# The opening of a diffusion mixer layer on one core: order of the first loads, and of TensorE's first steps

## The reference, cut to what matters

```
mod = silu(c) @ w_ada + b_ada                 # w_ada is (1024, 3072); one row for latent, one for context
shift, scale, gate = split(mod, 3)
h = rmsnorm(x, rms_g) * (1 + scale) + shift   # x is (tokens, 1024)
q, k, v, z_a, glu, z_b, gates = split(h @ w_in + b_in)
```

## Time and profile before

| | |
|---|---|
| median of 3 runs | 1721.22 us (1721.03 to 1722.77) |
| the profiled execution | 1720.91 us, of which its span is 1719.3 us |
| PE busy in the span | 1700.5 us (99%) |
| DVE, ACT, POOL busy | 1244.4, 866.7 and 653.4 us |
| granted clock of PE, mean | 0.999 |
| start of the first main product (line 1845) | 85.04 us |

### The profile page before, as it was taken

One profiled execution on the slowest core, in us unless ns is written; L12 is line 12 of the kernel. 1 busy time (PEld: TensorE's weight loads), 2 busy tenths in 40 slices (PEclk: granted clock), 3 DMA queues, 4 the chain that ended last, 5 costly groups with the idle time before them and its releaser, 6 DMA issues.

```text
span 1719.3 us, 27684 instructions
## 1 busy us (share of the span) xinstructions
PE 1700.5 (99%) x9909; PEld 1444.6 (84%) x9909; DVE 1244.4 (72%) x1791; ACT 866.7 (50%) x1508; POOL 653.4 (38%) x509
## 2 busy tenths in 40 slices
PE   8999999999999999999999999999999999999998
PEld 5787888888899988888888888888988888888886
DVE  3785888788757758887677856777777655678776
ACT  3553434454576644444554436777779222433443
POOL 0044676565200027865555653224223100015443
PEclk9999999999999999999999999999999999999999
DMA  9453534333598735444333369997666777673452
GB/s 325 127 158 118 140 122 145 92 89 111 182 325 247 212 92 141 156 120 111 99 129 99 110 169 220 245 209 192 167 143 173 247 239 227 195 258 133 150 159 86
DMA packets 271644, 286.31 MB, mean 167 GB/s; under 512 B 49960, under 2 KB 217748, under 8 KB 268309
## 3 DMA queue, kind: packets, MB, share of 16 engines
q1 hardware_dynamic: 271106, 284.18, 55.9%
q10 hardware_dynamic: 403, 0.37, 0.1%
HBM read 203.18 MB, written 81.30 MB: 165 GB/s over the span
## 4 chain that ended last, share of the span: by engine, by line
PE 94%; DMA 2%; DVE 1%; SPq 1%; issue 1%; POOL 1%; ACT 0%; POOLq 0%; DVEq 0%; ACTq 0%
PE banks L1845 45%; PE banks L2399 6%; PE banks L2974 4%; PE banks L2976 4%; PE banks L2975 4%; PE banks L3034 3%; PE banks L3036 3%; PE banks L3035 3%; PE banks L2363 3%; PE banks L1973 2%; PE banks L1975 2%; PE banks L1974 2%; PE banks L2369 2%; DMA w_ada<-in_w_ada 1%; PE banks L2339 1%; PE banks L2340 1%
## 5 line engine op out<-in xcount | busy, mean ns | idle before, releaser
L1845 PE MATMUL banks<-a_hi,w_hi 128*128 128x512 f32 x1176 | 460.7, 392 | 0.7 <-ACT out_stage L1122 0.4
L1845 PE MATMUL banks<-a_hi,w_lo 128*128 128x512 f32 x1176 | 458.3, 390 | 0.0
L1845 PE MATMUL banks<-a_lo,w_hi 128*128 128x512 f32 x1176 | 458.1, 390 | 0.0
L1514 DVE SCALAR_TENSOR_TENSOR banks<-glu_out,taps,banks 128x1009 f32<-128x1009 f32 (+1 forms) x240 | 342.2, 1426 | 5.2
L1845 PEld LDWEIGHTS banks<-a_hi,w_hi 128*128 128x128 f32 x1176 | 220.9, 188 | 50.0 <-issue 3.6
L1845 PEld LDWEIGHTS banks<-a_hi,w_lo 128*128 128x128 f32 x1176 | 220.9, 188 | 46.0
L1845 PEld LDWEIGHTS banks<-a_lo,w_hi 128*128 128x128 f32 x1176 | 221.0, 188 | 45.0
L1005 POOL TENSOR_TENSOR t_raw<-w_raw 128x512 f32<-128x512 f32 x39 | 53.8, 1380 | 397.7 <-DMA w_raw<-in_w_in 391.5
L1433 DVE SCALAR_TENSOR_TENSOR w_lo<-w_raw,w_hi 128x1024 fp32r<-128x1024 f32 x84 | 108.9, 1296 | 103.9 <-ACT w_hi L1096 102.6
L959 POOL TENSOR_TENSOR w_lo<-t_raw,w_hi 128x1024 fp32r<-128x1024 f32 x70 | 171.6, 2461 | 25.7 <-ACT w_hi L1096 23.3
L2511 ACT ACTIVATE probs<-scores,stat 128x640 f32<-128x640 f32 (+2 forms) x128 | 106.7, 833 | 52.3 <-DVE stat L2433 50.9
(11 more groups left out here) (286 smaller groups left out, 3687.5 us busy)
## 6 DMA issues: line engine op xcount, KB each, us to landing
w_raw<-in_w_in SPq DMA_DIRECT2D x34, 1024.0 KB, 5.6
cw_raw<-in_w_in SPq DMA_DIRECT2D x44, 512.0 KB, 5.0
proj<-out_stage SPq DMA_DIRECT2D x80, 256.0 KB, 2.3
gates_in<-proj SPq DMA_DIRECT2D x64, 256.0 KB, 3.0
k_hi<-k_hi_rows SPq DMA_DIRECT2D x16, 640.0 KB, 10.8
k_lo<-k_lo_rows SPq DMA_DIRECT2D x16, 640.0 KB, 13.3
q_split<-q_rows SPq DMA_DIRECT2D x8, 1152.0 KB, 6.2
w_ada<-in_w_ada SPq DMA_DIRECT2D x8, 1024.0 KB, 11.2
```

The costliest lines, as they stand in the source:

```text
L1514: op = dve.scalar_tensor_tensor(dst, src, by, dst, ALU.mult, ALU.add)
L1845: op = pe.matmul(out, x[w][:, b, k], y, start=(start and k == j == 0), stop=(k == H - 1 and j == 2), skip_group_check=not start)
```

## The change

Four hand-written orders are changed, and the filler transposes. No shape, buffer or arithmetic is changed.

- SP: the second half of the first chunk's rows is asked for right behind the first half, ahead of part 0 of w_ada. The weights of unit 1 are asked for ahead of part 1 of w_ada.
- ACT: `first_high(0)` goes behind the scaling of the fourth row tile, and `first_high(1)` ahead of `row_of(1)`.
- DVE: the third row tile is scaled ahead of `first_row`. The first part of `first_low(0)` goes ahead of `coefficients(0)`, its second part behind the first two splits, and `first_low(1)` follows whole, ahead of `coefficients(1)`.
- PE: the transposes of tiles 2 and 3 go ahead of `ada_products(0)`. The steps of blocks 0 and 1 with units 0 and 1 go ahead of `ada_products(1)`, and the turn of block 5 with them. Unit 2's steps of blocks 0 to 3 stand in one run behind `turn_row(2)`, followed by block 4 of units 0 and 1 ahead of `ada_products(3)`. There are 43 fillers in six places in this stretch where there were 27 in two places; they write another quarter of a bank, and 14 of them another bank.

```diff
--- before.py
+++ after.py
@@ -789,11 +789,11 @@
             sp.dma_start(c_rows[r:r + KC, :], a.rearrange("(r p) -> r p", p=P)).then_inc(start_in, 16)
         sp.dma_start(cst.ident[:], io.ident).then_inc(start_in, 16)
         load_x(sp, 0, 0)
+        load_x(sp, 0, 2)
         load_ada(0)
-        load_x(sp, 0, 2)
         load_first_w(0)
+        load_first_w(1)
         load_ada(1)
-        load_first_w(1)
         load_ada(2)
         load_first_w(2)
         load_ada(3)
@@ -1194,14 +1194,14 @@
         squares(0, 1)
         squares(0, 2)
         squares(0, 3)
-        first_high(0)
         act.wait_ge(xn_done, 2)
         act.wait_ge(rms_done, 5)
         act.activation(x_first[:, 3], x_first[:, 3], ACT.Copy, scale=rstd[:, 3:4]).then_inc(xn_done, 1)
+        first_high(0)
         modulate(0)
         modulate(1)
+        first_high(1)
         row_of(1)
-        first_high(1)
         modulate(2)
         modulate(3)
         first_high(2)
@@ -1570,15 +1570,15 @@
 
         normalize(0)
         columns()
+        normalize(1, (0,))
         first_row()
+        first_low(0, (0,))
         coefficients(0)
-        normalize(1, (0,))
-        first_low(0)
         split(0)
         split(1)
-        first_low(1, (0,))
+        first_low(0, (1,))
+        first_low(1)
         coefficients(1)
-        first_low(1, (1,))
         split(2)
         split(3)
         first_low(2)
@@ -1714,9 +1714,9 @@
         pe.wait_ge(start_in, 48)
         pe.transpose(ps_c, c_rows[:], cst.ident[0:2 * KC, 0:2 * KC]).then_inc(tr_done, 1)
 
-        def keep_busy(n):
+        def keep_busy(n, bank=4):
             for _ in range(n):
-                pe.transpose(banks[:, 4, 0:P], cst.ident[:], cst.ident[:])
+                pe.transpose(banks[:, bank, P:2 * P], cst.ident[:], cst.ident[:])
 
         keep_busy(6)
         pe.wait_ge(ada_out, 2)
@@ -1789,33 +1789,36 @@
         pe.wait_ge(rows_in, 16 * 7)
         pe.transpose(ps_rows, rows[0:R_C, :], cst.ident[0:R_C, 0:R_C]).then_inc(tr_done, 1)
         pe.transpose(ps_taps, taps[0:4 * TAPS, :], cst.ident[0:4 * TAPS, 0:4 * TAPS]).then_inc(tr_done, 1)
+        keep_busy(11)
+        for s in range(4):
+            first_turn(s, (2, 3)).then_inc(tr_done, 1)
         ada_products(0)
         keep_busy(3)
         turn_row(0)
-        keep_busy(24)
-        for s in range(4):
-            first_turn(s, (2, 3)).then_inc(tr_done, 1)
+        keep_busy(9)
         turn(4)
         pe.wait_ge(cols_done, 2)
         step(0, [0])
-        ada_products(1)
         step(1, [0])
-        turn_row(1)
         turn(5)
         step(0, [1])
         step(1, [1])
+        keep_busy(6)
+        ada_products(1)
+        keep_busy(4, 3)
+        turn_row(1)
+        keep_busy(10, 3)
         turn(6)
         step(2, [0, 1])
+        ada_products(2)
         step(3, [0, 1])
-        ada_products(2)
-        step(0, [2])
-        step(1, [2])
         turn_row(2)
-        step(2, [2])
-        step(3, [2])
+        for s in range(4):
+            step(s, [2])
+        step(4, [0, 1])
         ada_products(3)
         turn(7)
-        step(4, [0, 1, 2])
+        step(4, [2])
         turn_row(3)
         step(5, [0, 1, 2])
         step(6, [0, 1, 2])
```

## The result

The changed kernel takes 1724.81 us (median of 20 runs, 1722.44 to 1727.46) beside 1720.69 us for the kernel before (20 runs, 1720.2 to 1723.7). The ratio is 1.002, with a 95% interval from 1.0014 to 1.0026: 3.4 us slower, between 2.4 and 4.5. The forecast of 1723.0, or +1.8, had the sign, but the size is too small: its own range ended at +3.0. Only the wide range of 1719.9 to 1725.4, which leaves room for the rivals, holds the time. The profiled execution took 1726.43 us (span 1724.8) against 1720.91 (1719.3).

The account below looks back on a forecast made before the run. PE was taken as the bound; 1.1 us won at the start minus the hole before step 2 left 1.35 us late, 1.8 by step 6, hence 1723.0 us. Range 1719.9 to 1725.4, its own +0.8 to +3.0.

Parts of the forecast that it names:

- the rivals: Four other outcomes: head start kept (chance 0.12), cancelling out (0.25), PE at a slower pace (0.07), loads not moving (0.01).
- Loads: SP's queue: second rows land at 10.0 us, part 0 of w_ada at 16.6, part 1 at 26.85, later parts unchanged.
- Start of the steps: PE behind part 0 of w_ada: step 0 at 22.85 us against 23.93, 1.1 us earlier.
- Second group of steps and the six fillers: PE ahead of part 1: fillers take 0.6 us, `ada_products(1)` at 27.5, step 2 at 33.65, 2.3 us later.
- The ten fillers: PE ahead of step 2: free, covered by the wait for `modulate(2)`; without that wait they would cost 1.0 us.
- PE slows down: Rival: PE falls to half pace in the thin stretch from 27 to 33.6 us; +5, 1726.2 us; chance 0.07.
- From part 3 to step 8: `ada_products(3)` at 43.5 us, squares release `modulate(6)` last by 0.4, step 6 at 50.4 (1.8 late), step 8 at 57.6.
- Rest: each link is the same as before … nothing takes the 1.8 us back: Behind step 6: links of 2.39 and 4.84 us unchanged, then PE runs without a gap, so 1.8 us late remains.

Follow-up runs that it names:

- e10: The changed kernel without its six fillers ahead of `ada_products(1)`, the ten behind `turn_row(1)` kept: 1723.08 us, ratio 1.0012.
- e1: The changed kernel run again, unchanged: 1723.93 us, ratio 1.0019 to the kernel before.
- e6: The changed kernel without 16 fillers, six ahead of `ada_products(1)` and ten behind `turn_row(1)`: 1724.18 us, ratio 1.0019.
- e4: The kernel before with only SP's new order of loads: 1723.43 us, ratio 1.0016.
- e8: The kernel before, its loads kept, with `ada_products(2)` between steps 2 and 3 and the second half of the new step order: 1720.50 us, ratio 0.9998.
- e12: The kernel before with six extra subtractions on DVE ahead of `first_low(3)`, PE's stream unchanged: 1727.88 us, ratio 1.0040.
- e7: The kernel before with SP's new order of loads and 28 fillers ahead of `ada_products(0)`: 1722.87 us, ratio 1.0012.
- e2: The kernel before with 20 fillers ahead of step 8, a pure delay: 1724.92 us, ratio 1.0024.
- e5: The kernel before with three extra subtractions on DVE ahead of `first_low(3)`, PE's stream unchanged: 1724.15 us, ratio 1.0018.
- e11: The kernel before with the edits of e8 and e9 together: 1720.55 us, ratio 0.9999.
- e3: The kernel before with 16 more fillers, all put into gaps of PE in the opening: 1721.39 us, ratio 1.0003.
- e9: The changed kernel with ACT's `finish_part` moved ahead of the squares of the context rows near 450 us: 1723.11 us, ratio 1.0012.

## Why the prediction was right or wrong

**Loads: right, 0.35 us late.** The second rows are squared from 10.35 (10.0 predicted) and `ada_products(0)` starts at 16.98 (16.65). No step of PE waits for a later part of w_ada, as predicted, and the buffer wait of unit 2's weights cost nothing: SP issued them at 25.12 (25.05 before).

**Start of the steps: right.** Step 0 at 23.27 against 22.85. Of the 0.4 us, 0.3 is the landing's.

**Second group of steps and the six fillers: right.** `ada_products(1)` at 27.79 (27.5), behind six fillers at 27.04. The prediction put these six on the path, at 0.6 us; e10 against e1, with equal landings, shows 0.6.

**The ten fillers: right that they cost nothing, and the reason was short.** They stand ahead of a wait that ends later, as said. They do more: e6 against e10, one execution each, shows that without them the clock falls to 0.52 and step 2 runs at half pace. The rival "PE slows down" did not happen in the changed kernel (step 2's products start 0.23 apart) but its mechanism is real in e4, e6, e8 and e12, and far behind the opening in e7 and e10. Its price was put at 3 us for one stretch, which is too much: e4 paid 1.6 us in `ada_products(0)`, e7 and e10 1.6 each, and e6 reached step 8 1.15 us behind e10. A small slip beside it: the gaps of PE from 21 to 56 us add up to 3.45 us with the one of 0.28 us at 22.70, not to 3.2; nothing hangs on it.

**From part 3 to step 8: right.** `ada_products(3)` at 43.99 (43.5), step 6 at 50.70 (50.4), step 8 at 57.93 (57.6): each 0.3 to 0.5 late by the first landing. The squares are the last releaser of `modulate(6)`, as predicted: its coefficients were done at 48.39 and it started at 48.71, so they cost 0.3 us (0.4 predicted).

**"Rest: each link is the same as before … nothing takes the 1.8 us back": this is the term that failed.** It is true up to 400 us (315.00 of 315.00 us busy). Behind that the sum had zero, and the runs show 1.3 us by the ratio and 2.0 by the medians. Rows 1 ended at 400 us, and I took the rest from the same slack. The stages from 450 to 770 us have places where ACT or SP is released by a transfer whose landing isn't tied to PE's time, and where PE has only 1 to 2 us to spare before it must wait.

Three such transfers landed late in one execution or another: the context rows (after, e1, e10), `w_raw` at 634 us (e7) and `w_raw` at 753 us (e12). Twice, in e7 and e10, the wait was followed by half the granted clock, which nearly doubled its cost. e2 shows that a late start with 20 fillers, and none of the new order, brings an excess.

Whether the time or the added instructions bring it isn't settled. The last column of the table divides the kernels by PE's instructions rather than by the delay: with as many as before it is 0.0 to 0.4 us (e4, e5, e6, e8, e11; e12 apart), with 10 to 28 fillers more it is 0.2 to 3.7 (after, e1, e2, e3, e7, e9, e10). But e4, e5 and e6 have 0.7 to 1.1 by the medians, and at a delay of 2.1 to 2.3 us the intervals of the two groups overlap.

That the time came out inside the range is in part luck: the term of the sum that was wrong was covered by the room left for rivals that didn't happen.

**What stays open.** Why the context rows land in 7.7, 7.0, 6.4 and 7.7 us in after, e1, e2 and e10 and in 4.8 to 5.4 in the others. In these four the packet of the instruction queue (so named in the profile) near it lies at 448.3 to 449.2 us, 0.2 to 0.5 us ahead of the request, and takes 1.4 to 1.9 us; before, it lies at 452.2 and takes 0.96. That is a coincidence of times in single executions, and others speak against it: e3 has the packet 0.4 us ahead of the request, takes 0.94 and lands in 5.4; e9 has it 1.0 us ahead, takes 0.94 and lands in 5.0. The late `w_raw` of e7 has a packet of 0.94 us 0.7 us behind its request, but e2 and e3 have one 0.3 and 0.6 us behind theirs and land in 5.2 and 5.4. So a near packet alone isn't the cause.

Where it falls goes with PE's instructions: in the kernels with as many as before it lies 4.2 to 4.9 us behind the request of the context rows, in those with 10 to 20 fillers more 0.2 to 1.0 us ahead of it, and the four late landings are all among the latter. A run that adds instructions behind the opening, or as many as move the packet elsewhere, is missing.

That e9's order removes most of the excess is what its median and narrow spread suggest, not what an interval shows. The rest of 0.7 us in the profiled execution of the kernel after, between 590 and 1037 us, has no wait to its name and no fall of the clock.

## What to carry to other kernels

A stretch in which the bounding engine runs without a gap carries a delay unchanged, but only the stretch that was read does so: before a delay of the opening is priced at its own size, look through the rest of the program for places that wait for a transfer within a few microseconds, and at the granted clock behind each wait that is found. Read the excess in one execution, and in several: a median of many runs less a start that was read in one mixes two things. When fillers are weighed, ask of each two questions: is the wait behind it ended by something later (then it is free), and is it all that keeps the engine's clock up over the gap (then taking it out costs). And work queued behind a wait for a transfer, here `finish_part` behind the squares, passes the transfer's lateness on to whatever it feeds.

## What the runs showed of the hardware

The granted clock can differ between two executions of the same first 14 us. With a gap of 0.35 us ahead of the transposes (before) and of 0.96 (e11) `ada_products(0)` took 1.93 and 1.92 us; with 1.55 us (e8) and 1.43 us (e12) it took 3.45 and 3.48. The gap differed because the fillers ahead of it began to run at full pace at another moment.

Behind gaps of 3.18 (e4), 1.26 (e6), 2.02 (e10), 2.47 (e7 at 647 us) and 5.32 us (e12) the clock stood at 0.50 to 0.57, and it came back while PE worked. Behind gaps of 2.81 (e5) and 1.88 us (after, at 468 us) it stayed at 1.00. So in these runs the length of the gap alone doesn't say whether the clock falls. Behind e7's gap of 1.76 us ahead of the first transposes these kept their 1.09 us and, with 28 fillers after them, so did the products (1.92 us).
